# The decode tokens' GLA output, computed transposed, in a two-layer hybrid attention kernel

## The reference

```
qb = qc * exp(b)
att = where(causal, einsum('bhid,bhjd->bhij', qb, kc * exp(-b)), 0)
o   = einsum('bhij,bhjv->bhiv', att, vc) + einsum('bhid,bhdv->bhiv', qb, S)
o_g = o_g * rsqrt(mean(o_g * o_g, axis=-1) + EPS)          # over the 128 values of a head
o_g = o_g * gla_g * silu(rg)
x   = x + concat([o_g, o_s]) @ w_out
```

## Time and profile before

| | |
|---|---|
| median of 3 runs | 1941.1 us (1939.54 to 1942.73) |
| the profiled execution, its own time | 1939.54 us |
| its span in the profile | 1937.7 us |
| PE busy in the span | 1897.4 us, 98% |
| DVE busy | 1345.1 us, 69% |
| ACT busy | 1099.2 us, 57% |
| POOL busy | 1093.4 us, 56% |
| granted TensorE clock, mean | 0.997 of full speed |

### The profile page before, as it was taken

The page is one execution under the profiler, slowest core; times in us unless marked ns, Lnnn a source line. Parts: engine busy times, 40 slices in busy tenths (PEclk is TensorE's granted clock), DMA queues, the critical chain, the costliest instruction groups (busy, mean ns, idle before and its releaser), DMA issues.

```text
span 1937.7 us, 40813 instructions
## 1 busy us (share of the span) xinstructions
PE 1897.4 (98%) x15500; PEld 1870.2 (97%) x15500; DVE 1345.1 (69%) x2498; ACT 1099.2 (57%) x2228; POOL 1093.4 (56%) x811
## 2 busy tenths in 40 slices
PE   5999999999999999999999999999999999999997
PEld 5999999998999999999999999999998999999997
DVE  7976677576574986678578756874865568857774
ACT  4664566635445665566656646664353466645662
POOL 3666566732225666566766656676323366665763
PEclk9999999999999999999999999999999999999998
DMA  4233233331212232322323332324212222233331
GB/s 140 83 104 107 86 104 100 103 116 66 102 55 102 84 106 94 106 94 96 101 83 104 103 99 94 104 96 135 77 56 93 88 88 94 90 112 99 99 107 60
DMA packets 92114, 185.65 MB, mean 96 GB/s; under 512 B 12880, under 2 KB 22768, under 8 KB 91376
## 3 DMA queue, kind: packets, MB, share of 16 engines
q1 hardware_dynamic: 84096, 170.04, 26.7%
q10 hardware_dynamic: 7824, 13.00, 1.9%
HBM read 178.09 MB, written 6.95 MB: 95 GB/s over the span
## 4 chain that ended last, share of the span: by engine, by line
PE 93%; DVE 5%; ACT 1%; issue 1%; DMA 0%; POOLq 0%; POOL 0%; DVEq 0%; ACTq 0%
PE ps L822 57%; PE ps L782 22%; PE ps L831 7%; PE ps L1054 1%; PE ps L1043 1%; PE ps L810 1%; PE ps L1026 1%; DVE h_end L1711 1%; PE ps L1167 0%; DVE h_end L1714 0%; PE ps L802 0%; PE ps L1065 0%; DVE g_buf L2298 0%; DMA x<-xT 0%; DVE x L2360 0%
## 5 line engine op out<-in xcount | busy, mean ns | idle before, releaser
L822 PE MATMUL ps<-rhs,w_hi 128*128 128x272 f32 x4256 | 805.0, 289 | 0.0
L822 PEld LDWEIGHTS ps<-rhs,w_hi 128*128 128x128 f32 x4256 | 669.6, 188 | 0.6 <-DVE ssum L1901 0.5
L822 PE MATMUL ps<-rhs,w_lo 128*128 128x272 f32 x2128 | 614.1, 289 | 0.0
L659 POOL TENSOR_TENSOR w_lo<-w_raw,w_hi 128x512 fp32r<-128x512 f32 x272 | 350.9, 1295 | 248.4 <-ACT w_hi L1323 248.3
L822 PEld LDWEIGHTS ps<-rhs,w_lo 128*128 128x128 f32 x2128 | 402.3, 189 | 0.0
L653 POOL TENSOR_TENSOR w_lo<-w_raw,w_hi 128x1024 fp32r<-128x1024 f32 x80 | 190.9, 2388 | 347.8 <-ACT w_hi L1267 332.7
L822 PE MATMUL ps<-act_c,w_hi 128*128 128x272 f32 x1792 | 354.4, 289 | 1.1 <-DVE h_mid L1752 0.7
L659 POOL TENSOR_TENSOR w_lo<-s_tmp,w_hi 128x512 fp32r<-128x512 f32 x216 | 282.6, 1320 | 32.5 <-ACT w_hi L1323 32.3
L822 PEld LDWEIGHTS ps<-act_c,w_hi 128*128 128x128 f32 x1792 | 287.7, 188 | 1.8 <-DVE h_mid L1752 1.2
L782 PE MATMUL ps<-h_mid,w_hi 128*128 128x272 f32 x1600 | 276.6, 291 | 0.0
L822 PE MATMUL ps<-act_c,w_lo 128*128 128x272 f32 x896 | 258.3, 288 | 0.0
(11 more groups left out here) (291 smaller groups left out, 3161.0 us busy)
## 6 DMA issues: line engine op xcount, KB each, us to landing
w_raw<-stream SPq DMA_DIRECT2D x380, 256.0 KB, 2.9
w_raw<-stream SPq DMA_DIRECT2D x80, 512.0 KB, 3.3
g_buf<-stream SPq DMA_DIRECT2D x52, 256.0 KB, 2.8
pl_raw<-stream SPq DMA_DIRECT2D x64, 192.0 KB, 2.9
x<-xT ACTq DMA_DIRECT2D x8, 272.0 KB, 6.0
y_d<-x SPq DMA_DIRECT2D x8, 272.0 KB, 2.1
s<-s_d ACTq DMA_DIRECT2D x2, 1024.0 KB, 4.9
s_s_d<-s ACTq DMA_DIRECT2D x2, 1024.0 KB, 4.6
```

What stands on the lines that cost most here:

```text
L659: pool.tensor_tensor(operand(w_lo, j, half), source(op, s, half), operand(w_hi, j, half).bitcast(F32), ALU.subtract).then_inc(pool_low, 1)
L822: ins = pe.matmul(bank(s, at), w[:, k * P:(k + 1) * P], moving[:, k, side, r, :], start=fresh and k == 0 and w is hi and side == 0, stop=k ...
```

## The change

`gs_o` is computed the other way round: values on the partitions, 4 heads x 32 tokens along the free dimension. The weights of the matmuls are now the 128 columns of `v_tok` or `s0`; what moves is the scores (32 columns) or the queries of one sequence for two heads (8 columns). ACT copies the result out to `oS` in two parts, and DVE has no part in `gs_o`. The norm over the 128 values is now a sum over partitions, in new steps:

- `gsq` (slot 17): ACT squares `oS` into `sqS`.
- `gss` (slot 23): PE multiplies `sqS` with a column of ones, per head; ACT takes the root of the 32x4 result, DVE its reciprocal.
- `gbc` (slot 24): PE spreads the reciprocals over all partitions, per head. It stands in for the transpose `otr` 4 of slot 23.
- `gmix` 4 multiplies these by the gain and `oS` (4 instructions), and has one more multiplication by the gate.

`qd` becomes one tile of 128 columns. In the diff "..." marks what is left out.

```diff
             17: [("kv", 0), ("kv", 1)] + [("ssq", j) for j in range(4)] +
-                [("gs_o", 0), ("s_add", 0), ("att", 0)],
+                [("gs_o", 0), ("gsq", 0), ("s_add", 0), ("att", 0)],
...
-            23: [("gmix", 1), ("otr", 2), ("otr", 4)],
-            24: [("otr", 3), ("gmix", 2), ("klm", 0)],
+            23: [("gmix", 1), ("gss", 0), ("otr", 2)],
+            24: [("gbc", 0), ("otr", 3), ("gmix", 2), ("klm", 0)],
...
-        qd = [mx("qd0", [P, 2, NB * SAMP], 8 * U), mx("qd1", [P, 2, NB * SAMP], 13 * U + 8192)]
+        qd = mx("qd", [P, 2, NB, 2, NT], 15 * U + 4608)
...
+        def go_out():
+
+            return ps[:, 6, 0:4 * SAMP].rearrange("p (h b g t) -> p h b g t", h=2, b=NB, g=2)
...
-                            pe.matmul(ps[h * SAMP:(h + 1) * SAMP, 6, 0:P], atts[0:SAMP, hh, pr, :],
-                                      v_tok[0:SAMP, 4, h * P:(h + 1) * P], start=True, stop=False,
-                                      skip_group_check=True)
-
-                        for b in range(NB):
-                            for h in range(GH):
-                                pr, hh = divmod(h, 2)
-                                ins = pe.matmul(ps[h * SAMP:(h + 1) * SAMP, 6, 0:P],
-                                                qd[hh][:, pr, b * SAMP:(b + 1) * SAMP], s0[:, b, pr, :],
-                                                start=False, stop=b == NB - 1, skip_group_check=True)
+                            pe.matmul(go_out()[:, pr, :, hh, :], v_tok[0:SAMP, 4, h * P:(h + 1) * P],
+                                      atts[0:SAMP, hh, pr, :].rearrange("p (b t) -> p b t", t=NT),
+                                      start=h == 0, stop=False)
+
+                        for pr in range(2):
+                            for b in range(NB):
+                                ins = pe.matmul(go_out()[:, pr, b, :, :], s0[:, b, pr, :], qd[:, pr, b, :, :],
+                                                start=False, stop=pr == 1 and b == NB - 1)
...
-                    elif step == "otr" and i == NBLK:
-                        pe.wait_ge(m["o_out"], NBLK)
-                        pe.transpose(ps[:, 6, 0:P], oS[:, :], ident[:, :]).then_inc(m["gtr_done"], 1)
...
+                    elif step == "gss":
+                        pe.wait_ge(m["gsq"], 1)
+                        pe.wait_ge(m["o_out"], NBLK)
+                        for h in range(GH):
+                            ins = pe.matmul(ps[0:SAMP, 6, h:h + 1], sqS[:, h, :], ones[:, 0:1], start=True, stop=True)
+                        ins.then_inc(m["gss_done"], 1)
+                    elif step == "gbc":
+                        pe.wait_ge(m["g_recip"], 1)
+                        for h in range(GH):
+                            ins = pe.matmul(gla_out(NBLK)[0][:, h, :], rt[0:SAMP, h:h + 1].to_broadcast([SAMP, P]),
+                                            ident[0:SAMP, 0:SAMP], start=True, stop=True)
+                        ins.then_inc(m["gbc_done"], 1)
...
+                    elif step == "gss":
+                        act.wait_ge(m["gss_done"], 1)
+                        act.activation(rt[0:SAMP, 0:GH], ps[0:SAMP, 6, 0:GH], ACT.Sqrt, bias=eps[0:SAMP, :],
+                                       scale=1.0 / P).then_inc(m["g_root"], 1)
...
                     elif step == "gs_o":
                         act.wait_ge(m["go_done"], 1)
-                        act.activation(sqS[:, :], ps[:, 6, 0:P], ACT.Square,
-                                       accum_out=rt[:, 0:1]).then_inc(m["go_squared"], 1)
-                        act.wait_ge(m["go_squared"], 1)
-                        act.activation(rt[:, 0:1], rt[:, 0:1], ACT.Sqrt, bias=eps[:, :],
-                                       scale=1.0 / P).then_inc(m["go_root"], 1)
+                        for hh in range(2):
+                            ins = act.activation(oS[:, hh:4:2, :].rearrange("p h (b t) -> p h b t", t=NT),
+                                                 go_out()[:, :, :, hh, :], ACT.Copy)
+                        ins.then_inc(m["go_out"], 1)
...
+                    elif step == "gsq":
+                        act.wait_ge(m["go_out"], 1)
+                        act.activation(sqS[:, :, :], oS[:, :, :], ACT.Square).then_inc(m["gsq"], 1)
...
+                        link(dve.memset(qd[:, :, :, :, :], 0.0))
                         for hh in range(2):
-                            link(dve.memset(qd[hh][:, :, :], 0.0))
                             rows = slice(hh * HD, (hh + 1) * HD)
-                            first, last = qd_data(hh)
-                            dve.tensor_copy(first, qG[rows, :, SEQ:T - NT].rearrange("p h (b t) -> p h b t", t=NT))
-                            dve.tensor_copy(last, qG[rows, :, T - NT:T]).then_inc(m["q_paired"], 1)
+                            ins = dve.tensor_copy(qd[rows, :, :, hh, :], qG[rows, :, SEQ:T]
+                                                  .rearrange("p h (b t) -> p h b t", t=NT))
+                        ins.then_inc(m["q_paired"], 1)
...
-                    elif step == "gs_o":
-                        dve.wait_ge(m["go_root"], 1)
-                        link(dve.reciprocal(rt[:, 0:1], rt[:, 0:1]))
-                        dve.tensor_scalar(oS[:, :], ps[:, 6, 0:P], rt[:, 0:1], None, ALU.mult).then_inc(m["go_out"], 1)
+                    elif step == "gss":
+                        dve.wait_ge(m["g_root"], 1)
+                        dve.reciprocal(rt[0:SAMP, 0:GH], rt[0:SAMP, 0:GH]).then_inc(m["g_recip"], 1)
...
+                            dve.wait_ge(m["gbc_done"], 1)
+                            for h in range(GH):
+                                ins = dve.scalar_tensor_tensor(out=out[:, h, :], in0=out[:, h, :],
+                                                               scalar=lp[:, GG + h:GG + h + 1], in1=oS[:, h, :],
+                                                               op0=ALU.mult, op1=ALU.mult)
+                            link(ins)
+                            ins = dve.tensor_tensor(out, out, rG[:, :, cols], ALU.mult)
```

More of the change, by code:

```diff
@@ L312, in trunk @@
         m_swa = mx("m_swa", [P, 2 * WIN], off)
-        oS = mx("oS", [P, P], off)
+        oS = mx("oS", [P, GH, SAMP], off)
         off += 1024
@@ L317, in trunk @@
         m_samp = mx("m_samp", [P, WIN + SAMP], off)
-        sqS = mx("sqS", [P, P], off)
+        sqS = mx("sqS", [P, GH, SAMP], off)
         off += 640
@@ L507, in trunk @@
                    "ga_out", "go_done", "go_out", "klm_made", "fourfold", "s0_scaled", "gkv_done", "gkv_used", "r_silu",
-                   "go_squared", "go_root", "gtr_done", "ssq", "s_added", "ssum_done", "s_root", "q_paired",
+                   "gsq", "gss_done", "g_root", "g_recip", "gbc_done", "ssq", "s_added", "ssum_done", "s_root", "q_paired",
                    "mix_made", "mix_high", "mix_ready", "o_squared", "o_root", "otr_done", "gmix_made", "gmix_high", "gmix_ready", "kb_made"]
@@ L1193, in mixer @@
                         pe.wait_ge(m["v_out"], 5)
-                        pe.wait_ge(m["q_paired"], 2)
+                        pe.wait_ge(m["q_paired"], 1)
                         for h in range(GH):
                             pr, hh = divmod(h, 2)
-                            pe.matmul(ps[h * SAMP:(h + 1) * SAMP, 6, 0:P], atts[0:SAMP, hh, pr, :],
-                                      v_tok[0:SAMP, 4, h * P:(h + 1) * P], start=True, stop=False,
-                                      skip_group_check=True)
-                        for b in range(NB):
-                            for h in range(GH):
-                                pr, hh = divmod(h, 2)
-                                ins = pe.matmul(ps[h * SAMP:(h + 1) * SAMP, 6, 0:P],
-                                                qd[hh][:, pr, b * SAMP:(b + 1) * SAMP], s0[:, b, pr, :],
-                                                start=False, stop=b == NB - 1, skip_group_check=True)
+                            pe.matmul(go_out()[:, pr, :, hh, :], v_tok[0:SAMP, 4, h * P:(h + 1) * P],
[5 more added lines that the diff above has]
+                                                start=False, stop=pr == 1 and b == NB - 1)
                         ins.then_inc(m["go_done"], 1)
@@ L2316, in mixer @@
                             dve.wait_ge(m["otr_done"], i + 1)
-                        else:
[L2318 to L2322, removed]
+                            for h in range(GH):
+                                ins = dve.scalar_tensor_tensor(out=out[:, h, :], in0=out[:, h, :],
+                                                               scalar=lp[:, GG + h:GG + h + 1], in1=rG[:, h, cols],
+                                                               op0=ALU.mult, op1=ALU.mult)
+                        else:
+                            dve.wait_ge(m["gbc_done"], 1)
+                            for h in range(GH):
+                                ins = dve.scalar_tensor_tensor(out=out[:, h, :], in0=out[:, h, :],
```

(4 more changed lines are left out.)

## The result

The change makes the kernel slower: 1954.55 us (median of 6 runs, 1953.36 to 1957.73) against 1941.2 us before (median of 6), a ratio of 1.0072 with a 95% interval of 1.0059 to 1.0085. That is 13.4 us. The direction was forecast, the size was not: the forecast was +6 us.

What follows compares the result with a forecast made beforehand. The prediction took PE as the bound. A layer: +3.6 us of new PE work, -1.8 for the old wait, +1.2 for the table load, +3.0; two layers +6.0, so 1947 us, range 1943 to 1950.

Steps and rivals of the forecast that it cites:

- the first paragraph: What bounds the kernel: PE, busy 1897.4 of 1937.7 us at full clock, idling 1.80 us before `att` 1.
- part 1: `gs_o` on PE: the swapped matmuls take 4.6 us instead of 2.24, +2.4 us a layer (+2.3 to +2.7).
- the rivals: Hidden table load, 1944.7, chance 0.25; cheap swap on PE, 1938.7, chance 0.08; new wait at `gbc`, 1948.5, chance 0.12.
- the term of `gs_o`: PE's time for the swapped `gs_o` matmuls: 4.6 us after, 2.24 before, so +2.4 us a layer.
- The 8 records on 32 rows: The 4 `gs_o` matmuls with 32x128 weights and 32 moving columns: 0.125 us a record, 1.0 us in all.
- The estimate from weight columns: `gs_o` weight loads at columns divided by 1.2 ns: 1.9 us before, 4.3 after, a difference of +2.3.
- Part 2: `gss` +0.35 us and `gbc` +1.0 on PE, less 0.10 for transpose `otr` 4: +1.25 us a layer.
- Part 3: Wait before `att` 1: DVE starts `s_add` 2.3 us earlier, PE comes 2.4 later; wait gone, -1.8 us a layer.
- Part 4: The 1.28 us table load moves to block 0's root, giving PE a new 1.2 us wait before `kv` 4.
- Part 5: The chain `gss`, root, reciprocal, `gbc`: ready just when PE wants it, costed at nothing, up to 0.3 us.
- one with a lower price: Swap cheap on PE: 8-column matmuls at 30 ns a record, giving 1938.7, or 1936.3 with table load hidden; chance 0.08.

Runs made afterwards that it cites:

- 64 columns: The changed kernel with each of the 16 state matmuls of `gs_o` moving 64 columns, 56 of them zeros, instead of 8: 1947.58 us, ratio 1.0032.
- the pieces: The changed kernel with the `gs_o` matmuls, still 8 moving columns, split in four and spread over job 17: 1954.51 us, ratio 1.0064.
- the later scaling: The kernel before with only GpSimd's scaling of `s0` moved one weight tile later: 1936.53 us, ratio 0.9977.
- the early root: The changed kernel with an added, unread square root on ACT behind `gsq`, pulling the table load to slot 17: 1952.31 us, ratio 1.0046.
- both repairs: The changed kernel with 64 moving columns (56 of them zeros) and the added early square root on ACT: 1945.5 us, ratio 1.0020.
- the added matmuls: The kernel before with 16 unread matmuls, 128x128 weights and 8 moving columns, added ahead of those of `gs_o`: 1950.3 us, ratio 1.0043.

## Why the prediction was wrong

**The step that failed** is in the first paragraph and in part 1: "the clock at its full level, 2.4 GHz, in all slices". The trace bore that out for the kernel before; the step that failed was to carry it over to the kernel after. I read the granted clock in the kernel before and took it for a constant. All durations of part 1 came from rows at that level, and none of the rivals had another one. So the term of `gs_o`, +2.4, was too small, and the dense work behind it, `att` 0 and job 18, had no term at all. The run with 64 columns shows that this is the whole of it there: at full clock the group takes 3.72 us where the forecast had 3.6. The low clock cost 5.71 - 3.72 = 2.0 us on it and 9.14 - 6.50 = 2.6 us on `att` 0 and job 18, 4.6 us in layer 0. In layer 1 it cost less: 4.82 - 3.72 = 1.1 us on the group and 1.9 us behind it, 3.0 in all. The profiled execution took 1954.67 us, 15.1 over the one profiled before, 9.1 over the forecast's +6.0. From the starts of the same groups of PE in the two traces, 7.8 us of the 15.1 were lost in the mixer of layer 0, 6.2 in that of layer 1, and 1.0 between the two. The forecast had 3.0, 3.0 and nothing. So the low clock accounts for 4.6 + 3.0 = 7.6 of the 9.1, and 1.0 more is the open point below. In the medians the miss is 13.4 - 6 = 7.4 us.

**Part 1's other durations** were right. A record with wide weights costs 113 ns by forecast and 116 with 64 columns at full clock; with 8 columns, in the pieces, 101 to 115 (0.81 us for 8 in the second piece, 0.92 in the first). The 8 records on 32 rows took 1.01 us for a forecast of 1.0. The estimate from weight columns beside it, 1.9 us before and 4.3 after, was low on both sides: the traces have 2.24, and 3.72 + 1.01 = 4.73 at full clock. Only its difference fits.

**Part 2** was right: 0.34 and 1.00 us, and 0.09 us back for the transpose.

**Part 3** was right in its size and incomplete in its cause. The wait went. But 1.5 us of it did not need the change: they came from DVE's addition overlapping GpSimd's scaling, as the run with the later scaling shows. The other 0.3 went when DVE no longer stood still for the root.

**Part 4** was right: 1.1 us for 1.2 in layer 0 and 1.0 in layer 1, at the place named, and the early root takes it away. No drain was seen behind the load: 545.54 + 1.28 = 546.82, and the root begins at 546.83.

**Part 5** was right: nothing waits at `gbc`.

**The rivals.** None came true. None of them let a record cost more than at full clock: for the 8-column records there was one with a lower price, 30 ns, and none with a higher one.

What stays open: PE spends 1.0 us more between the two mixers than before, with no idle and a full clock, in the changed kernel and in the one with both repairs alike (from the last `gs_kv` group of layer 0 to slot 16 of layer 1). No run was made on it. Why the low spell differs from execution to execution is not settled either. That it does is seen at a place which the change does not touch, the first norm's 12 records with one moving column. In four of the ten profiled executions (64 columns, the early root, the added matmuls, the four pieces) the clock fell within 1 us behind them, for about 3 us, and all that follows came 1.3 to 1.6 us later; in the other six, the kernels before and after among them, it stayed at 1.00. PE in the run with 64 columns:

```profile
31.00:34.00 3.00, 3.00 (x16) 0.51 0.02 5
```

PE had also been idle several times for a few tenths of a us just before, in the kernel before as in these, so this is no test of the small records alone. It does show that executions of these kernels can differ by such a spell, whatever the change does.

## What to carry to other kernels

A row of matmuls that keeps PE busy but moves few columns can cost the clock, as it did here, and then the dense work behind it pays too: before small matmuls are put in a row, ask what moves, keep the narrow side as the weights, or put dense work between them, and look at the clock in short stretches, as the mean over the mixer (0.98) hardly shows it. A wait whose releaser is named should be followed one step further, to why the releaser was late; here an overlap of two engines was most of it, and changing one condition won what the change could not. When an activation leaves its place, follow its table load to the next one that needs the table.

## What the runs showed of the hardware

- Moving 64 columns instead of 8 made the same 32 records faster, 3.72 against 5.71 us, as the clock stayed at 2.4 GHz and did not fall to 1.2. The Trainium skill (TensorE: Matmul & The Clock Gate, What's actually happening) says that the gate follows how busy PE has been lately. The trace agrees that recent work sets it, but PE was busy without a gap when it fell.
- DVE additions with two SBUF inputs took 2.32 and 2.33 us in place of 0.72 while GpSimd worked on SBUF, and GpSimd's two scalings took 4.76 us in place of 3.8. The Trainium skill (GPSIMD Engine Reference, Specifications) names the SBUF interfaces that the two share, and contention for DVE instructions with two SBUF inputs; the trace agrees. In that run both engines lost time; in the kernel before only DVE did (2.25 us, with 3.81 for GpSimd).
